# A hybrid diffusion layer on one core: fp32r buffers spaced off multiples of 256 bytes, and a feed-forward block whose two activation parts lie side by side

## The reference

```python
D_MODEL = 2048; SEQ = 256; CTX_LEN = 256; D_FF = 5632

def _swiglu(h, w1, w3, w2):
    return (jax.nn.silu(h @ w1) * (h @ w3)) @ w2

x = x + 0.5 * mx[2] * _swiglu(_modulate(_rmsnorm(x, norm_ffn1), mx[0], mx[1]), ffn1_w1, ffn1_w3, ffn1_w2)
y = y + 0.5 * mc[2] * _swiglu(_modulate(_rmsnorm(y, norm_ffn1), mc[0], mc[1]), ffn1_w1, ffn1_w3, ffn1_w2)
...   # context projection, HGRN2 heads, Hyena heads, output projection w_out: x changes, y is done
x = x + 0.5 * mx[8] * _swiglu(_modulate(_rmsnorm(x, norm_ffn2), mx[6], mx[7]), ffn2_w1, ffn2_w3, ffn2_w2)
out = _rmsnorm(x, final_norm)
```

## Time and profile before

| | us |
|---|---|
| median of 3 runs | 3269.48 (3268.39 to 3271.21) |
| the profiled execution, on the device | 3267.79 |
| its span, first to last instruction | 3264.4 |
| PE busy | 3164.5 (97%) |
| DVE busy | 2035.5 (62%) |
| ACT busy | 1176.1 (36%) |

### The profile page before, as it was taken

How to read it: one execution, slowest core, us unless ns; L and a number is a source line. 1 busy time by engine, 2 the same in 40 slices (tenths; PEclk the granted TensorE clock), 3 DMA queues, 4 the chain that set the end, 5 groups by cost and what they waited for, 6 DMA issues and landing times. The chain is left out here.

```text
span 3264.4 us, 49834 instructions
## 1 busy us (share of the span) xinstructions
PE 3164.5 (97%) x19388; PEld 2786.1 (85%) x19388; DVE 2035.5 (62%) x2657; ACT 1176.1 (36%) x1534; POOL 133.5 (4%) x173
## 2 busy tenths in 40 slices
PE   6979999999999999999998999999998999999998
PEld 3338888888888888888877999999998999999998
DVE  5567746558465675655447767776656555555556
ACT  3132121222222222222236777753334443444444
POOL 1000000000000000000000023330000000000000
PEclk8999999999999999999998999999999999999999
DMA  7647544535446676665323554445544555555653
GB/s 260 224 169 216 165 154 142 180 129 177 147 139 219 194 249 217 216 211 173 97 90 123 162 174 150 148 148 185 157 149 152 183 181 183 183 180 180 185 182 128
DMA packets 438914, 563.28 MB, mean 173 GB/s; under 512 B 17855, under 2 KB 395064, under 8 KB 437896
## 3 DMA queue, kind: packets, MB, share of 16 engines
q1 hardware_dynamic: 432208, 545.80, 53.1%
q0 software_dynamic: 2816, 9.43, 0.9%
q10 hardware_dynamic: 3768, 6.37, 0.6%
HBM read 553.14 MB, written 8.39 MB: 172 GB/s over the span
## 5 line engine op out<-in xcount | busy, mean ns | idle before, releaser
L405 DVE TENSOR_TENSOR w_lo<-raw,w_hi 128x1024 fp32r<-128x1024 f32 x736 | 912.3, 1242 | 938.8 <-ACT w_hi L400 935.2
L400 ACT ACTIVATE w_hi<-raw 128x1024 fp32r<-128x1024 f32 x736 | 775.0, 1057 | 1425.2 <-PE bank L417 1403.8
L415 PE MATMUL bank<-h_hi,w_hi 128*128 128x512 f32 (+1 forms) x2816 | 952.7, 338 | 23.0 <-DVE h_lo L483 19.9
L416 PE MATMUL bank<-h_lo,w_hi 128*128 128x512 f32 (+1 forms) x2816 | 950.8, 338 | 0.0
L417 PE MATMUL bank<-h_hi,w_lo 128*128 128x512 f32 (+1 forms) x2816 | 950.4, 337 | 0.0
L415 PEld LDWEIGHTS bank<-h_hi,w_hi 128*128 128x128 f32 x2816 | 538.1, 191 | 79.8 <-issue 15.5
L417 PEld LDWEIGHTS bank<-h_hi,w_lo 128*128 128x128 f32 x2816 | 537.9, 191 | 56.0
L416 PEld LDWEIGHTS bank<-h_lo,w_hi 128*128 128x128 f32 x2816 | 538.1, 191 | 55.3
L415 PE MATMUL bank<-g_hi,w_hi 128*128 128x512 f32 (+1 forms) x1408 | 475.4, 338 | 5.3 <-DVE g_lo L789 4.7
L416 PE MATMUL bank<-g_lo,w_hi 128*128 128x512 f32 (+1 forms) x1408 | 474.2, 337 | 0.0
L417 PE MATMUL bank<-g_hi,w_lo 128*128 128x512 f32 (+1 forms) x1408 | 474.1, 337 | 0.0
(11 more groups left out here) (244 smaller groups left out, 2767.6 us busy)
## 6 DMA issues: line engine op xcount, KB each, us to landing
raw<-in_ffn_w_dram SPq DMA_DIRECT2D x528, 512.0 KB, 3.6
ada_raw<-in_ada_w_dram SPq DMA_DIRECT2D x260, 512.0 KB, 4.5
raw<-in_w_in_dram SPq DMA_DIRECT2D x176, 512.0 KB, 3.8
raw<-in_w_out_dram SPq DMA_DIRECT2D x32, 512.0 KB, 3.6
ada_over<-in_ada_w_dram SPq DMA_DIRECT2D x28, 512.0 KB, 4.8
spec<-spec_spill POOLq DMA_DIRECT2D x8, 768.0 KB, 5.1
spec_spill<-spec_out ACTq DMA_DIRECT2D x4, 1280.0 KB, 5.1
xin<-in_x_dram SPq DMA_DIRECT2D x1, 2048.0 KB, 9.7
```

Source lines behind the costliest of these rows:

```text
L400: nc.scalar.activation(w_hi[un.slot(j)][:], raw[un.slot(j)][:], ACT.Copy).then_inc(hi_done, 1)
L405: nc.vector.tensor_tensor(w_lo[un.slot(j)][:], raw[un.slot(j)][:], w_hi[un.slot(j)][:].bitcast(F32), ALU.subtract).then_inc(lo_done, 1)
L415: nc.tensor.matmul(o, w_hi[slot][:, c0:c0 + P], hi, start=start, stop=False, skip_group_check=True)
L416: nc.tensor.matmul(o, w_hi[slot][:, c0:c0 + P], lo, start=False, stop=False, skip_group_check=True)
```

## The change

Three things change. A new helper `spaced` makes a list of tiles with an unused gap behind each; with it the ring's weight buffers and the activations of both feed-forward blocks get different distances from multiples of 256 bytes. `w_hi` a to d now start 128, 192, 0 and 64 bytes past one, `w_lo` 128, 64, 0 and 192; the 16 tiles of `h1_hi`, `h1_lo` and `h2` step by 32 bytes, the four of `g1_hi`, `g1_lo` and `g2_both` by 64. The mixer's activations stay at 128. `rows` moves to another place in SBUF for room; `h1` is now one tile for each of 16 feature blocks, with latent and context tokens next to each other.

In the second block `hi` and `lo` of an activation lie side by side in one tile (`h2`, `g2_both`). `two_pass` replaces the trio: `w_hi` times both at once, 512 columns into a whole bank, and `w_lo` times `hi`, 256 columns into its first half. The result is now the sum of a bank's two halves. ACT copies the second half of the w1 and w3 banks to SBUF, DVE adds the first (`usum`, and `vsum` in `gmul`); silu and the product then work in SBUF. In `add` DVE adds the two halves one after the other, and the second waits for the first (`badd`).

```diff
+        def spaced(name, count, shape, gap, scope=life):
+            made = []
+            for n in range(count):
+                letter = "abcdefghijklmnop"[n]
+                made.append(sb(f"{name}_{letter}", shape, F32R, scope=scope))
+                sb(f"{name}_gap_{letter}", [P, gap], scope=scope)
+            return made
...
-        w_hi = [sb(f"w_hi{s}", [P, UNIT], F32R) for s in range(RING)]
+        w_hi = spaced("w_hi", RING, [P, UNIT], 16)
-        w_lo = [sb(f"w_lo{s}", [P, UNIT], F32R) for s in range(RING)]
+        w_lo = spaced("w_lo", RING, [P, UNIT], 48)
...
-        h1_hi = sb("h1_hi", [P, 2, KB, SEQ], F32R, scope=ffn)
-        h1_lo = sb("h1_lo", [P, 2, KB, SEQ], F32R, scope=ffn)
-        g1_hi = [sb(f"g1_hi{b}", [P, 512], F32R, scope=ffn) for b in range(FBLK)]
-        g1_lo = [sb(f"g1_lo{b}", [P, 512], F32R, scope=ffn) for b in range(FBLK)]
+        h1_hi = spaced("h1_hi", KB, [P, 2, SEQ], 8, ffn)
+        h1_lo = spaced("h1_lo", KB, [P, 2, SEQ], 8, ffn)
+        g1_hi = spaced("g1_hi", FBLK, [P, 512], 16, ffn)
+        g1_lo = spaced("g1_lo", FBLK, [P, 512], 16, ffn)
...
+        h2 = spaced("h2", KB, [P, 2, SEQ], 8, f2)
+        g2_both = spaced("g2_both", FBLK, [P, 2, SEQ], 16, f2)
+        g2_hi = [g[:, 0] for g in g2_both]
+        g2_lo = [g[:, 1] for g in g2_both]
+        g2_up = [g[:, SEQ:2 * SEQ] for g in g1]
...
+        def two_pass(o, slot, c0, hi, both, start, stop):
+            nc.tensor.matmul(o, w_hi[slot][:, c0:c0 + P], both, start=start, stop=False, skip_group_check=True)
+            return nc.tensor.matmul(o[:, 0:SEQ], w_lo[slot][:, c0:c0 + P], hi, start=False, stop=stop, skip_group_check=True)
...
         def up_bank(b, ntok):
-            return bank[b][:, 0:ntok] if ntok == 512 else bank[b // 2][:, b % 2 * 256:(b % 2 + 1) * 256]
+            return bank[b][:]
...
+            def silu_sum(sub, c):
+                for n in range(2 * sub, 2 * sub + 2):
+                    ac.wait_ge(s["usum"], c * FBLK + (n + 1))
+                    nc.scalar.activation(g[n], g[n], ACT.Silu).then_inc(s["silu"], 1)
+            def v_copy(un, j, sub, c):
+                ac.wait_ge(w_used, used(un, j))
+                for b in range(2):
...
+                    nc.scalar.activation(g2_up[n], bank[2 + b][:, SEQ:2 * SEQ], ACT.Copy).then_inc(s["vcopy"], 1)
...
+                    else:
+                        ve.wait_ge(s["vcopy"], c * FBLK + (n + 1))
+                        nc.vector.tensor_tensor(g2_up[n], g2_up[n], bank[2 + b][:, 0:SEQ], ALU.add).then_inc(s["vsum"], 1)
...
+            def usum(un, j, sub, c):
+                ve.wait_ge(w_used, used(un, j))
+                for b in range(2):
+                    n = 2 * sub + b
+                    ve.wait_ge(s["ucopy"], c * FBLK + (n + 1))
+                    nc.vector.tensor_tensor(g[n], g[n], bank[b][:, 0:SEQ], ALU.add).then_inc(s["usum"], 1)
...
+                        for n in range(2):
+                            if n:
+                                ve.wait_ge(s["badd"], c * KB + (d + 1))
+                            ins = nc.vector.scalar_tensor_tensor(
+                                out=res[0][:, d, :], in0=bank[downs[d % len(downs)]][:, n * 256:(n + 1) * 256],
+                                scalar=gate[:, gt, d, 0:1], in1=res[0][:, d, :], op0=ALU.mult, op1=ALU.add)
```

More of the change, by code:

```diff
@@ L208, in build @@
         window = sb("window", [P, TB, HY], scope=first)
+        rows = [sb(f"rows{n}", [P, P], scope=first) for n in range(4)]
         fw1 = sb("fw1", [FILT_EMB, FILT_ORDER], scope=first)
@@ L361, in build, with ffn_sems @@
         mod_done = sem("mod_done")
-        def ffn_sems(tag):
-            return {n: sem(f"{tag}_{n}") for n in ("silu", "gmul", "ghi", "glo", "bdone", "bfree")}
-        fa, fb_ = ffn_sems("ffn1"), ffn_sems("ffn2")
+        def ffn_sems(tag, more=()):
+            return {n: sem(f"{tag}_{n}") for n in ("silu", "gmul", "ghi", "glo", "bdone", "bfree") + more}
+        fa, fb_ = ffn_sems("ffn1"), ffn_sems("ffn2", ("ucopy", "vcopy", "usum", "vsum", "badd"))
         def chain_sems(tag, names):
@@ L417, in three_pass, with both_unit @@
             return nc.tensor.matmul(o, w_lo[slot][:, c0:c0 + P], hi, start=False, stop=stop, skip_group_check=True)
+        def two_pass(o, slot, c0, hi, both, start, stop):
+            nc.tensor.matmul(o, w_hi[slot][:, c0:c0 + P], both, start=start, stop=False, skip_group_check=True)
+            return nc.tensor.matmul(o[:, 0:SEQ], w_lo[slot][:, c0:c0 + P], hi, start=False, stop=stop, skip_group_check=True)
+        def both_unit(pe, un, j, kg, outs2, hi, both):
+            pe.wait_ge(lo_done, un.number(j) + 1)
+            for k in range(4):
+                kb = 4 * kg + k
+                for b in range(2):
+                    last = two_pass(outs2[b], un.slot(j), k * 256 + b * P, hi(kb), both(kb), kb == 0, kb == KB - 1)
+            last.then_inc(w_used, 1)
         def col_unit(pe, un, j, kg, outs2, hi, lo, shared):
@@ L687, in up @@
                     if not (isinstance(c, int) and c == 0 and sub == 0):
-                        pe.wait_ge(s["gmul"] if part else s["silu"], c * FBLK + (2 * sub))
-                col_unit(pe, un, j, kg, [out(2 * part), out(2 * part + 1)], hi, lo, ntok == 256)
+                        free = ("gmul" if part else "silu") if ntok == 512 else ("vsum" if part else "usum")
+                        pe.wait_ge(s[free], c * FBLK + (2 * sub))
+                if ntok == 512:
+                    col_unit(pe, un, j, kg, [out(2 * part), out(2 * part + 1)], hi, lo, False)
+                else:
+                    both_unit(pe, un, j, kg, [out(2 * part), out(2 * part + 1)], hi, lo)
             def down(un, j, jj, c):
@@ L701, in down @@
                     for f in range(FBLK):
-                        last = three_pass(bank[downs[d % len(downs)]][:, 0:ntok], un.slot(j), f * 256 + q * P,
-                                          g_hi[f][:], g_lo[f][:], f == 0, f == FBLK - 1)
+                        o, c0 = bank[downs[d % len(downs)]][:], f * 256 + q * P
+                        if ntok == 512:
+                            last = three_pass(o, un.slot(j), c0, g_hi[f][:], g_lo[f][:], f == 0, f == FBLK - 1)
+                        else:
+                            last = two_pass(o, un.slot(j), c0, g_hi[f], g_lo[f][:], f == 0, f == FBLK - 1)
                     last.then_inc(w_used if q else s["bdone"], 1)
@@ L742, in silu @@
                         ac.wait_ge(s["glo"], c * FBLK + (2 * sub + b + 1 - FBLK))
-                    nc.scalar.activation(g[2 * sub + b], up_bank(b, ntok), ACT.Silu).then_inc(s["silu"], 1)
+                    if ntok == 512:
+                        nc.scalar.activation(g[2 * sub + b], up_bank(b, ntok), ACT.Silu).then_inc(s["silu"], 1)
+                    else:
+                        nc.scalar.activation(g[2 * sub + b], bank[b][:, SEQ:2 * SEQ], ACT.Copy).then_inc(s["ucopy"], 1)
+            def silu_sum(sub, c):
[6 more added lines that the diff above has]
+                    n = 2 * sub + b
+                    if not (isinstance(c, int) and c == 0):
+                        ac.wait_ge(s["gmul"], c * FBLK + (n + 1 - FBLK))
+                    nc.scalar.activation(g2_up[n], bank[2 + b][:, SEQ:2 * SEQ], ACT.Copy).then_inc(s["vcopy"], 1)
             def ghi(sub, c):
```

49 lines of the change are left out of this document (32 added, 17 removed).

## The result

| | us |
|---|---|
| kernel before, median of 7 runs | 3269.48 (3266.10 to 3273.40) |
| changed kernel, median of 7 runs | 3279.52 (3276.93 to 3285.87) |
| ratio, with its 95% interval | 1.0031 (1.0021 to 1.0042) |

The changed kernel is slower by 0.31%. The prediction, 3250 with a range up to 3262, was wrong. The profiled execution of the changed kernel took 3278.71 us.

What follows compares the result with a forecast made beforehand. The prediction took PE's matmul pace, with 13.3 ns fixed per fp32r matmul, as the bound. Terms -26.9 + 1.2 + 6.4 = -19.3 us against the profiled 3267.8 gave 3248.5, so a median of 3250, range 3190 to 3262.

Steps and rivals of the forecast that it cites:

- The distances: All fp32r matmuls: new offsets between tiles modulo 256 bytes change nothing; bounds were nothing or 10.6 ns either way.
- The distances lift part or all of the 13.3 ns: Rival, both feed-forward blocks and mixer: new distances cut the fp32r matmul's fixed price; 3123 us, half of it 3187; chance 0.22.
- The distances make reads worse: Rival, both feed-forward blocks: 2 ns on 6336 + 4224 matmuls loses all, 10.6 ns gives 3362 us; chance 0.04.
- The pair's price: Second block: matmuls of 512 and 256 columns cost 226.7 + 120.0 = 346.7 ns, against 360.0 for a trio.
- the two passes: Second block: a pair replacing a trio saves one fixed price, 13.3 ns, on 2016 trios: 26.9 us.
- The fixed price is not one per instruction: Rival, second block: only 2.7 ns saved per trio, 5.4 us won and 7.6 lost, 3272 us; chance 0.03.
- DVE's unit of 2.96 us: Second block's down units: DVE needs 1.14 + 1.82 = 2.96 us a unit with doubled adds, against PE's 2.77.
- the margin of 0.4 us: Second block's down units: DVE adds block 10 at 19.0 us, PE wants its bank at 19.4; priced at nothing.
- DVE takes the down units: Rival, second block: dependent add pairs 0.1 us dearer give about 3258 us, chance 0.06; 0.2 or 0.3 us dearer, chance 0.03.
- The end of the block: Second block's last down units: doubled adds cost 6.4 us, and one copy and two sums ahead add 1.2 us.
- the sum without the distances: Whole kernel: -26.9 + 1.2 + 6.4 = -19.3 us, giving a median of 3250, with the distances taken as nothing.

Runs made afterwards that it cites:

- e1_side_only: The changed kernel with all gaps at zero, so every distance is 0 again; side-by-side parts and two passes stay: 3251.83 us, ratio 0.9947 to the kernel before.
- e11_order: Adds unused series of 60 matmuls, some mixing distances or widths, on TensorE alone after the kernel's work; 512 columns: 226.7 ns at distance 0, 233.2 at 128.
- e5_same_64_128: `e1_side_only` with h1 and h2 shifted 64 bytes against the weights, g1 and g2 128, the mixer's activations 64: 3280.63 us, ratio 1.0027 to the kernel before.
- e10_series: Adds to the kernel with zero gaps unused series of 48 matmuls on TensorE alone, after its work; 512 columns: 226.7 ns at distance 0, 233.4 at 128.

## Why the prediction was wrong

**What failed** is "The distances": "I take nothing." In the whole kernel it is +27.7 us (3279.5 less the 3251.8 of `e1_side_only`), and it turns -17.6 into +10.0. The argument was that a clash by address should vary, while 18 starts and 5836 were alike. But the prediction's own sentence ahead of it said that all tiles of before lie at one distance, and the description of the kernel that every slice lies a multiple of 256 further on. If the price goes by distance, that kernel cannot vary. Equal paces spoke as little against the idea as for it. A short series at each of two distances is enough to see the difference: 226.7 and 233.4 ns.

The failed term was also bounded unevenly. I took the rival "The distances lift part or all of the 13.3 ns" for 0.22 and "The distances make reads worse" for 0.04, because the change seemed to start from a bad place. It started, for 512 columns, from the best of the places tried: 13.3 ns over the columns at 0, up to 20.8 at 160. The rival's own figure was 2 ns on 10560 matmuls to lose all. Measured against `e1_side_only`, 5.2 ns on 6336 lose 33 us and 2.5 ns on each of 2112 pairs 5. The 4992 between the blocks (the prediction's 3072 leave out the context and the output projection) are 2.2 to 3.2 ns faster, 12 us by their paces, of which the stage shows 6.5 (763.9 to 757.4) while PE idles 4.3 us more in it. Together that is some 32 us lost, against 27.7 measured; the rest isn't accounted for.

**What held.** The pair's price: 346.7 ns forecast, 346.3 to 346.7 in `e1_side_only`, though it splits as 230.1 + 116.6 and not as 226.7 + 120.0; the sum was right, its parts were not. That was in part luck. By `e11_order` the sum isn't a law: a pair at distance 0 can also take 353.5 ns, and by that price the two passes would have saved 6.5 ns a trio, half of what was forecast. The rival "The fixed price is not one per instruction", with 2.7 ns saved, is out for this kernel. DVE's unit of 2.96 us held, and so did the margin of 0.4 us, which is tightest where the pair is fastest: in `e1_side_only` too PE is busy for 400.00 of the 400 us from 2600 to 3000 us. With that the rival "DVE takes the down units" is out. The end of the block: 7.2 us of waits for 7.6, of which `x_res` has 4.5 and not 5 to 6. And the sum without the distances: 3250 against 3251.8 for the kernel without its gaps.

At half clock the distances do nothing, as the earlier trace rows had it for distance 0. The first pairs of the second block in the changed kernel, distances of two tiles:

```profile
2503.18 0.63 PE L431 MATMUL bank<-h_a,w_hi_a 128*128 128x512 f32 x1
...
2505.10 0.63 PE L431 MATMUL bank<-h_c,w_hi_a 128*128 128x512 f32 x1
```

Three pairs in 1.92 us, 640 ns each: 768 columns at 1.2 GHz and nothing over. These are distances 0 and 32, which don't differ for a pair at full clock either. In `e5_same_64_128`, where the same pairs have distance 64 and take 353.3 ns at full clock, three of them take 1.92 us at half clock as well:

```profile
2511.60 0.63 PE L438 MATMUL bank<-h_b,w_hi_a 128*128 128x512 f32 x1
...
2513.52 0.63 PE L438 MATMUL bank<-h_c,w_hi_a 128*128 128x512 f32 x1
```

## What to carry to other kernels

When all rows of a trace share a property, they say nothing about its price: either measure it with a short series of its own, or give both signs the same weight and let the range reach as far on the slow side as on the fast one. Let the series have the kernel's own order of widths, and check it in the kernel: the pair at distance 0 had one price here and another there. A nanosecond on each of the changed kernel's 15,552 matmuls with fp32r weights is 15.6 us, so the unknown that touches every instruction is worth more care than the 27 us that were counted row by row. And when a change has two parts, run each alone: here one was worth -17.6 us and the other hid it.

## What the runs showed of the hardware

- The time of an fp32r matmul with its own weight load depends on how far the streamed data and the weights lie apart modulo 256 bytes. For 512 columns 0 is the best (226.7 ns, 13.3 over its columns), 64 is 228.9, the other multiples of 32 are 233.4 to 234.1 (`e10_series`), and 4 bytes are 236.7. For 256 columns 0 is the dearest of the multiples of 32, beside 96 and, in `e11_order`, 128 (120.0 ns each), and 192 reaches 113.3 (`e11_order`); 8 bytes are worse, 126.7.
- It does so with every other engine and all DMAs idle (`e10_series`, 3288 to 3585 us). The Trainium skill, TensorE: Matmul & The Clock Gate, "Step-by-step: what each phase is for", says that weight loads have a read port of their own and don't take bandwidth from the running matmul; the series, in which the distance between the two is all that changes, differ by 6.7 ns of 226.7. That fits the statement badly, but doesn't refute it: whether it is the reads that clash, or something behind them, was not shown.
- Shorter loads don't lower the price in step: at distance 0 256 columns go from 120.0 to 113.3 ns with 64 columns of weights and stay there with 32, and 512 columns go up from 226.7 to 230.2 and 231.7.
- Prices of neighbours don't simply add (pairs 346.7 to 353.7 ns, matmuls in the pattern 64, 64, 192 at 233.3 where the parts give 230.4), and one distance can have two steady paces (a pair at 0: 346.7 and 353.5; 256 columns at 192: 117.8 and 113.3).
